# Beginning three output tiles of a retention layer before its last head is normalised

## The reference, cut to what matters

```python
o = o.transpose(1, 0, 3, 2, 4).reshape(B, S, H, dv)        # H = 4 heads, dv = 512
mu = jnp.mean(o, axis=-1, keepdims=True)
var = jnp.mean(jnp.square(o - mu), axis=-1, keepdims=True)
o = ((o - mu) * lax.rsqrt(var + LN_EPS)).reshape(B, S, H * dv) * gn_g.astype(f32)
y = (jax.nn.silu(g.astype(f32)) * o).astype(h.dtype)
return y @ w_out                                           # (512, 2048) @ (2048, 1024)
```

## Time and profile before

| | |
|---|---|
| median of 3 runs | 2953.64 us (2951.76 to 2955.32) |
| the profiled execution | 2953.68 us, span 2951.9 us |
| PE busy | 2858.2 us, 97% of the span |
| DVE, ACT, POOL busy | 47%, 33%, 16% |
| mean granted TensorE clock | 0.990 of full speed |

### The profile page before, as it was taken

How to read it: one execution, slowest core, us unless ns; L and a number is a source line. 1 busy time by engine, 2 the same in 40 slices (tenths; PEclk the granted TensorE clock), 3 DMA queues, 4 the chain that set the end, 5 groups by cost and what they waited for, 6 DMA issues and landing times. The chain is left out here.

```text
span 2951.9 us, 37772 instructions
## 1 busy us (share of the span) xinstructions
PE 2858.2 (97%) x14556; PEld 2353.7 (80%) x14556; DVE 1376.6 (47%) x1827; ACT 983.6 (33%) x1571; POOL 474.3 (16%) x363
## 2 busy tenths in 40 slices
PE   7999999998999999999999997999999999999998
PEld 5888888887876688888877875888888788888887
DVE  4464543335557754333445555443334465443333
ACT  4322432225145543222322323332223433332222
POOL 0021122100111212221011221022210012022210
PEclk9999999999999999999999998999999999999999
DMA  4323233333510023333232221233332332233331
GB/s 146 93 85 94 70 107 95 96 100 107 142 44 1 1 65 107 99 90 101 85 100 79 85 67 55 86 93 97 93 98 90 103 90 86 79 93 99 98 93 59
DMA packets 459669, 256.07 MB, mean 87 GB/s; under 512 B 9632, under 2 KB 447632, under 8 KB 459424
## 3 DMA queue, kind: packets, MB, share of 16 engines
q1 hardware_dynamic: 455488, 246.50, 28.5%
q10 hardware_dynamic: 3456, 5.77, 0.7%
q0 software_dynamic: 608, 2.16, 0.2%
HBM read 248.11 MB, written 2.10 MB: 85 GB/s over the span
## 5 line engine op out<-in xcount | busy, mean ns | idle before, releaser
L1443 DVE TENSOR_TENSOR w_lo<-w_raw,w_hi 128x1024 fp32r<-128x1024 f32 x461 | 626.0, 1359 | 943.9 <-ACT w_hi L1058 943.4
L478 PE MATMUL acc<-a_hi,w_hi 128*128 128x512 f32 x2264 | 890.1, 393 | 8.3 <-DVE y_lo L1899 5.1
L480 PE MATMUL acc<-a_hi,w_lo 128*128 128x512 f32 x2264 | 880.0, 389 | 0.0
L479 PE MATMUL acc<-a_lo,w_hi 128*128 128x512 f32 x2072 | 807.0, 389 | 0.0
L1058 ACT ACTIVATE w_hi<-w_raw 128x1024 fp32r<-128x1024 f32 x461 | 483.5, 1050 | 521.6 <-PE acc L480 462.5
L478 PEld LDWEIGHTS acc<-a_hi,w_hi 128*128 128x128 f32 x2264 | 426.2, 188 | 101.1 <-issue 12.8
L480 PEld LDWEIGHTS acc<-a_hi,w_lo 128*128 128x128 f32 x2264 | 425.6, 188 | 88.4
L479 PEld LDWEIGHTS acc<-a_lo,w_hi 128*128 128x128 f32 x2072 | 389.7, 188 | 79.8 <-issue 1.4
L480 PE MATMUL acc<-hid_hi,w_lo 128*128 128x512 f32 (+1 forms) x704 | 264.5, 376 | 0.0
L479 PE MATMUL acc<-hid_lo,w_hi 128*128 128x512 f32 (+1 forms) x704 | 264.5, 376 | 0.0
L478 PE MATMUL acc<-hid_hi,w_hi 128*128 128x512 f32 (+1 forms) x704 | 264.5, 376 | 0.0
(11 more groups left out here) (302 smaller groups left out, 3484.7 us busy)
## 6 DMA issues: line engine op xcount, KB each, us to landing
w_raw<-ffn_w_gate SPq DMA_DIRECT2D x88, 512.0 KB, 3.8
w_raw<-ffn_w_up SPq DMA_DIRECT2D x88, 512.0 KB, 3.8
w_raw<-gm_w_in SPq DMA_DIRECT2D x64, 512.0 KB, 4.0
w_raw<-ffn_w_down SPq DMA_DIRECT2D x64, 512.0 KB, 3.8
w_raw<-ret_w_in SPq DMA_DIRECT2D x48, 512.0 KB, 3.8
w_raw<-gm_w_out SPq DMA_DIRECT2D x32, 512.0 KB, 3.7
w_raw<-ffn_w_down SPq DMA_DIRECT2D x32, 384.0 KB, 3.3
w_raw<-nsa_w_in SPq DMA_DIRECT2D x21, 512.0 KB, 3.9
```

Source lines behind the costliest of these rows:

```text
L478: pe.matmul(o_bank, lhs_hi, rhs_hi, start=start, stop=False)
L479: pe.matmul(o_bank, lhs_hi, rhs_lo, start=False, stop=False)
L480: return pe.matmul(o_bank, lhs_lo, rhs_hi, start=False, stop=stop)
L1443: dve.tensor_tensor(w_lo[:, slot, :, :], w_raw[:, slot, :, :], w_hi[:, slot, :, :].bitcast(f32), ALU.subtract).then_inc(lo_done, 1)
```

## The change

On PE the output projection no longer starts with unit 0 behind `norm_mean`. Parts of units 0 to 4 that need only heads 0 to 2 are made first: k-steps 0 to 3 of unit 0 ahead of `norm_mean`; the rest of unit 0, unit 2 and the first half of unit 1 ahead of `norm_var`; the first half of unit 3 and unit 4 behind it. The second halves of units 1 and 3, which need head 3, come last. Then `dense` goes on from unit 5. `unit_done` is counted up by two at the end of unit 1 and by two at the end of unit 3, so that units 2 and 4, though done, hold their slots until then.

On DVE the last head is taken out of the loop too, and the low parts of y tiles 0 to 7 are made two by two ahead of its four copies to `ro`. Low parts 8 to 11 come behind `centre`, then the low parts of units 3 and 4, then the variance. On ACT unit 3 is split between y tiles 7 and 8, and unit 4 behind the squares of head 3. `residual` no longer makes these two splits.

```diff
--- before.py
+++ after.py
@@ -388,6 +388,8 @@
 
             return st[:, :, :] if s % 2 == 0 else acc[:, 1:3, :]
 
+        OUT_BEGUN = [L["n_out"] for L in PL if L["kind"] == 2]
+
         block = ctx.enter_context(nc.Block())
 
 
@@ -1004,13 +1006,32 @@
                                              start=m == 0, stop=m == CH - 1)
                         last.then_inc(ro_done, 1)
                 loop(pe, RH, head, 1)
+
+                def part(j, k0, k1, then=0):
+
+                    n, o, t = L["n_out"] + j, L["o_out"] + j // 2, j % 2
+                    pe.wait_ge(lo_done, n + 1)
+                    if t == 0:
+                        wait(pe, acc_free, o - BANKS + 1)
+                    for k in range(k0, k1):
+                        kk = t * KMAX + k
+                        pe.wait_ge(y_lo_done, kk + 1)
+                        last = product(acc[:, o % BANKS, :], w_hi[:, n % SLOTS, k, :], w_lo[:, n % SLOTS, k, :], tile(y_hi, kk), y_lo[:, kk, :],
+                                       kk == 0, kk == 2 * KMAX - 1)
+                    if then:
+                        last.then_inc(unit_done, then)
+
+                part(0, 0, 4)
                 norm_mean(RH)
-
-                def last_var(i, j):
-                    if isinstance(i, int) and i == 0 and j == 0:
-                        norm_var(RH)
-
-                dense(L["n_out"], L["o_out"], 2, 8, TWO, y_hi, y_lo, after=last_var, operand=(y_lo_done, 0), tail_of=L["b_mid"])
+                part(0, 4, 8, then=1)
+                part(2, 0, 8)
+                part(1, 0, 4)
+                norm_var(RH)
+                part(3, 0, 4)
+                part(4, 0, 8)
+                part(1, 4, 8, then=2)
+                part(3, 4, 8, then=2)
+                dense(L["n_out"], L["o_out"], 2, 8, TWO, y_hi, y_lo, begun=5, tail_of=L["b_mid"])
 
 
             pe.wait_ge(params, 16)
@@ -1085,7 +1106,8 @@
                     act.dma_start(t_pos[:, :], positions[0, :].partition_broadcast(P)).then_inc(pos_in, 16)
                 for t in range(DT - 1):
                     for j in range(t * G, t * G + G):
-                        split_unit(n0 + j + AHEAD)
+                        if t or n0 not in OUT_BEGUN:
+                            split_unit(n0 + j + AHEAD)
                     act.wait_ge(unit_done, n0 + t * G + G)
 
                     wait(act, ss_sum, DT * (b - 1) + t)
@@ -1401,9 +1423,11 @@
                     act.wait_ge(unit_done, L["n_out"])
                     act.wait_ge(ry_done, 4 * RH - 4)
                     split_y(0, 8)
+                    split_unit(L["n_out"] + AHEAD)
                     act.wait_ge(rs_done, 4 * RH)
                     split_y(8, 12)
                     squares(RH)
+                    split_unit(L["n_out"] + AHEAD + 1)
                     act.activation(r4[:, 7:8], ones[:, 0:1], ACT.Sqrt)
                     act.wait_ge(r_var_rd, RH)
                     act.activation(r_sd[:, :], r_sd[:, :], ACT.Sqrt).then_inc(r_root, 1)
@@ -1889,18 +1914,21 @@
                             dve.scalar_tensor_tensor(rp[m][:, :], acc[:, (o0 + m) % BANKS, 0:SEQ - m * P], R_QK ** -0.5,
                                                      decay[:, i, 0:SEQ - m * P], ALU.mult, ALU.mult).then_inc(acc_free, 1)
                         for e in range(4):
+                            if isinstance(i, int) and i == RH - 1:
+                                split_y(2 * e, 2 * e + 2)
                             dve.wait_ge(ro_done, i * 4 + (e + 1))
                             dve.tensor_copy(ro[:, e, :], acc[:, (o0 + e) % BANKS, :]).then_inc(acc_free, 1)
-                    loop(dve, RH, head, 1)
 
                     def split_y(t0, t1):
                         for t in range(t0, t1):
                             dve.wait_ge(y_hi_done, t + 1)
                             dve.tensor_tensor(y_lo[:, t, :], ry[:, t, :], y_hi[t].bitcast(f32), ALU.subtract).then_inc(y_lo_done, 1)
+                    loop(dve, RH, head, 1, 1)
                     centre(RH)
-                    split_y(0, 8)
+                    split_y(8, 12)
+                    split_unit(L["n_out"] + AHEAD)
+                    split_unit(L["n_out"] + AHEAD + 1)
                     variance(RH)
-                    split_y(8, 12)
                     finish_head(RH)
                     split_y(12, 16)
                 residual(L["b_mid"])
```

## The result

The changed kernel takes 2936.28 us (median of 5 runs, 2934.95 to 2937.12), the kernel before 2951.76 us (5 runs, 2949.88 to 2955.32) beside it: ratio 0.9946, 95% interval 0.9933 to 0.9959, so 15.5 us or 0.54% faster. The forecast was 2937.4 us, with a range of 2934 to 2943.

The account below looks back on a forecast made before the run. PE, 97% busy, bounds the kernel; 22.3 us lost around head 3. Losses left: 1.3 mean, 3.3 gap, 0.8 clock, 0.45 unit 5, with handovers 6.0; saved 16.3, so 2953.7 becomes 2937.4 us, range 2934 to 2943.

Parts of the forecast that it names:

- last copy late by: DVE's fourth copy to `ro`: starts 1.85 us late, as low parts and POOL's additions hold each other.
- sum of the mean: PE makes k-steps 0 to 3, waits 1.3 us for POOL's third addition; sum ends 1.8 us later than before.
- sum of the variance: PE makes 16 k-steps (10.9 us) first, so the sum starts at 1805.9, against 1805.62 before.
- variance to reciprocal: DVE, low parts 8 to 11 gone from between: reciprocal 1.4 us behind the variance instead of 3.01.
- gap ahead of head 3's rows: PE, after 12 k-steps behind the variance, idles from 1815.1 to 1818.4, 3.3 us.
- unit 5 starts: PE starts unit 5 at 1825.1 instead of 1841.43, with 0.8 us for clock and 0.45 us for a new stall.
- Low parts between the copies: DVE: two low parts fit each gap, but alternate with POOL's additions for head 3; the first two pairs cost nothing.
- The clock: PE behind the 3.3 us gap: low clock costs 0.8 us, between bounds of 0 and 2.6.
- the one of no effect: Rival, chance 0.04: low parts 0 to 3 not ready when PE asks; 0 to 3 us saved, 2952.
- the slower one: Rival, chance 0.04: held slots starve units 5 to 15 of splits, 35 us added, 2972.
- the exclusion: DVE subtractions and POOL additions block each other; rival, chance 0.12: costs nothing and clock holds, 18 to 18.5 us saved.
- the colder one: Rival, chance 0.18: PE's clock falls twice and head 3's chain is later; 11 to 12.5 us saved, 2942.

Follow-up runs that it names:

- a2: The changed kernel run again unedited, as base for other runs: 2937.08 us, ratio 0.9948 to the kernel before.
- e3: Changed kernel with low parts 0 to 3 ahead of the first copy, 4 and 5 ahead of the second, 6 and 7 behind the fourth: 2935.54 us.
- e5b: Changed kernel with PE summing the variance ahead of the first half of unit 1, not behind it: 2934.04 us, ratio 0.9937 to the kernel before.
- e1: Changed kernel with low parts 0 to 7 again behind the centring and all of unit 0 behind the mean's sum: 2945.61 us.
- e2: Changed kernel without units 3 and 4 begun ahead of head 3's rows (20 k-steps begun instead of 32): 2945.24 us.
- e5: Changed kernel with the variance summed ahead of unit 1's first half and low parts 8 to 11 between variance and reciprocal: 2934.45 us.

## Why the prediction was right

Point by point, in us behind the end of head 3's output:

| step | forecast | measured |
|---|---|---|
| last copy late by | 1.85 | 1.48 |
| sum of the mean | 4.05 | 3.67 |
| sum of the variance | 16.05 | 15.55 |
| variance to reciprocal | 1.4 | 1.39 |
| gap ahead of head 3's rows | 3.3 | 3.35 |
| PE goes on | 28.55 | 28.13 |
| unit 5 starts | 35.25 | 36.73, and 34.23 in a2 |

- *Low parts between the copies.* The alternation came as drawn: POOL's first two additions were held (1.65 and 1.58 us instead of 1.26), and then low parts 5 and 7 by them. Each of the two pairs made the copy behind it 0.74 us later, where I had drawn 1.0 and 0.85. e3 showed the cause by moving the low parts and nothing else.
- *The skill's rule.* That a VectorE instruction with two SBUF inputs and a GpSimd one that reads SBUF exclude each other, as the Trainium skill says ("SBUF — State Buffer", section "Who interferes with whom"), agrees with these rows. So does its free case, an instruction of VectorE with at most one input from SBUF (outside its 2-port modes): the copy of the first output tile, whose input is PSUM, ran beside an addition of POOL's, and they took 0.69 and 1.29 us, where they take 0.69 and 1.27 alone (rows of the changed kernel).

```profile
1823.17 0.69 DVE L1495 COPY F<-acc 128x512 f32<-128x512 f32 x1 [4.47 <-ACT sq L1114]
1823.22 1.29 POOL L1959 TENSOR_TENSOR SS<-SS,sq 128x512 f32<-128x512 f32 x1 [16.41 <-ACT sq L1114]
```

- *The variance.* PE's order set it, not POOL's sums, by 1.7 us; e5b showed that DVE is next, 0.7 us on.
- *The clock.* This was the mis-sized term: I took 0.8 us, and the gap cost 2.5 us in the first profile, nothing in a2's, and 1.6 and 1.4 us in e1 and e3. Up to unit 5, 14.9 us were saved in the first profile and 17.4 in the second, and 16.3 was the forecast.
- *Unit 5.* 0.26 us at the low clock, 0.43 at full clock, for 0.45 forecast.
- *Behind it.* No wait for a weight came in units 6 to 15 in the first profile, so the held slots starve nothing. The rest of the profiled span, outside the 51.6 and the 36.7 us, is 1.6 us shorter after. I have no cause in the change for that: 0.9 us of it lies ahead of head 3's output, which starts at 1780.95 before and 1780.02 after, and between 1778.06 and 1781.40 in the other profiles.
- *Luck in the number.* 2936.3 us lies 1.1 us from the forecast, but in part by luck. The forecast started from 2953.7 us, and the kernel before took 2951.8 beside the changed one; against that, 15.5 us were saved where I said 16.3. The two profiled executions differ by 16.6 us, nearly the forecast, only because the 1.6 us without a cause made up for the clock, which cost 1.7 us more there than I took.

Of the rivals, the one of no effect is refuted by PE's rows, the slower one by the waits; the exclusion did cost time; and the colder one came half true (the clock at the restart, fully in the first profile and in part in e1 and e3) without the rest of it.

## What to carry to other kernels

Where PE stands still for a chain on other engines, draw the chain with its times and count how many k-steps are free of it: work begun there counts in full (12 k-steps of 8.2 us were worth 8.2 and 9.0 us in medians), until the gap is full. Ask then what the work needs and where its operands are made, since that costs on the chain: VectorE subtractions from SBUF are cheap between two copies only while GpSimd is idle (1.28 us for two, against 2.36), and the same eight placed elsewhere cost 1.1 us less. Don't leave a gap like the one of 3.35 us here in front of dense matmuls if there is anything to put in it: half a weight unit was worth 5.7 and 6.5 us in medians, and 3.1 us of the stretch even against the execution that had kept its clock.

## What was unexpected of the hardware

- A gap of PE of 3.35 us was followed by a low clock (1.2 GHz) over the next 12 matmuls in one execution, and by none in another of the same program (3.34 us); in e1 and e3 it was 8 and 6 matmuls. The low clock came behind every gap of 5.07 us or more here, and it didn't last longer for a longer gap: behind 11.55 us (e2) it was 8 matmuls. It came behind no gap of 0.97, 0.63 or 1.55 us ahead of head 3's rows. The length of a single gap doesn't decide it: in e5 gaps of 0.57 and 1.47 us on both sides of the variance's sum (PE busy 1.15 of 3.2 us, second row) were followed by the low clock too (first row), while in the kernel before a gap of 1.48 us behind that sum, with none ahead of it, was not the earlier trace rows:

```profile
1804.70:1808.00 3.30, 3.30 (x9) 2.54 (x8) 3.30 (x3) 0.00 (x0) 0.00 (x0) 0.50 0.41 124
1801.00:1804.20 3.20, 1.15 (x4) 0.33 (x3) 2.90 (x4) 2.25 (x4) 1.07 (x2) 1.00 0.22 59
```

- GpSimd gets its turn between two subtractions of VectorE that follow each other without idle time. The prediction had drawn it so, and the rows bear it out: low part 4 started at 1785.25 and low part 5 at 1785.85, POOL's addition came in between (1785.41, 1.65 us), and low part 5 took 1.76 us.
